# Gate matrix of a PEER layer: one of four weighted one-hot rows made on ScalarE instead of VectorE

## What is computed

```
expert_idx = take_along_axis(cand_idx, pos)      # i1 * 128 + i2, 8 x 16 = 128 pairs a token
gate = softmax(top_s)
u = w_down[expert_idx]
act = gelu(einsum("td,thkd->thk", x, u)) * gate
y = einsum("thk,thkd->td", act, w_up[expert_idx])
```

## Time and profile before

| what | value |
|---|---|
| median of 3 runs | 3774.1 us (3767.93 to 3777.16) |
| profiled execution | 3774.63 us, span 3772.9 us |
| mean granted clock of TensorE | 0.913 |
| gate matrix stage | first comparison at 1072.75 us, last Gelu ends at 1256.55 us |
| busy over the span | TensorE 3206.5 us, VectorE 2896.3 us, ScalarE 1722.9 us, GpSimd 938.3 us |

### The profile page before, as it was taken

How to read it: one execution, slowest core, us unless ns; L and a number is a source line. 1 busy time by engine, 2 the same in 40 slices (tenths; PEclk the granted TensorE clock), 3 DMA queues, 4 the chain that set the end, 5 groups by cost and what they waited for, 6 DMA issues and landing times. The chain is left out here.

```text
span 3772.9 us, 47355 instructions
## 1 busy us (share of the span) xinstructions
PE 3206.5 (85%) x16065; PEld 2717.1 (72%) x16065; DVE 2896.3 (77%) x3965; ACT 1722.9 (46%) x1905; POOL 938.3 (25%) x566
## 2 busy tenths in 40 slices
PE   4877559688888799999999756569999999999991
PEld 4877437588888788888888425457888887877881
DVE  5899673358979787787888233569999999998995
ACT  3222222323333333333333122168787888877782
POOL 4455100034521254444444000110101101111112
PEclk8888779899999899999999876589999999999996
DMA  3121002224344799898997201279999999998983
GB/s 104 45 67 34 1 10 102 95 95 145 132 163 179 287 354 345 328 333 338 347 343 272 93 9 51 82 278 351 358 357 361 348 355 363 356 366 349 357 341 127
DMA packets 198884, 851.15 MB, mean 226 GB/s; under 512 B 21232, under 2 KB 104960, under 8 KB 155584
## 3 DMA queue, kind: packets, MB, share of 16 engines
q1 hardware_dynamic: 170288, 698.66, 50.3%
q0 software_dynamic: 28496, 151.16, 9.9%
HBM read 808.20 MB, written 59.38 MB: 230 GB/s over the span
## 5 line engine op out<-in xcount | busy, mean ns | idle before, releaser
L2468 DVE TENSOR_TENSOR moe_w_lo<-all_raw,moe_w_hi 128x2048 fp32r<-128x2048 f32 x298 | 674.2, 2284 | 74.0 <-ACT moe_w_hi L2412 73.5
L2412 ACT ACTIVATE moe_w_hi<-all_raw 128x2048 fp32r<-128x2048 f32 x298 | 565.8, 1914 | 44.2 <-PE moe_GU L2383 29.7
L2383 PE MATMUL moe_GU<-moe_w_hi,moe_x_lo 128*128 128x512 f32 x1056 | 418.1, 396 | 0.0
L2381 PE MATMUL moe_GU<-moe_w_hi,moe_x_hi 128*128 128x512 f32 x1056 | 417.9, 396 | 0.0
L2382 PE MATMUL moe_GU<-moe_w_lo,moe_x_hi 128*128 128x512 f32 x1056 | 417.9, 396 | 0.0
L463 DVE SCALAR_TENSOR_TENSOR all_yT<-proj_gated,proj_taps,all_yT 128x512 f32<-128x512 f32 x240 | 266.4, 1110 | 8.5
L1100 POOL TENSOR_TENSOR score_wd_lo<-all_hT,score_wd_hi 128x1024 fp32r<-128x1024 f32 x52 | 139.5, 2709 | 528.5 <-ACT score_wd_hi L1147 528.5
L1618 DVE SCALAR_TENSOR_TENSOR experts_pair<-experts_pair,all_x_first 128x1024 f32<-128x1024 f32 x128 | 156.3, 1221 | 141.3 <-DMA experts_pair<-in_peer_pairs,experts_slot 141.3
L1467 POOL DMA_INDIRECT experts_pair<-in_peer_pairs,experts_slot x128 | 223.6, 1747 | 115.4 <-POOL experts_slot L1464 109.6
L1464 POOL COPY experts_slot<-all_pair_id 128x1 uint32 x128 | 153.3, 1197 | 331.5 <-DVE all_h L1630 300.4
L2382 PEld LDWEIGHTS moe_GU<-moe_w_lo,moe_x_hi 128*128 128x128 f32 x1056 | 198.8, 188 | 48.6
(11 more groups left out here) (442 smaller groups left out, 8382.7 us busy)
## 6 DMA issues: line engine op xcount, KB each, us to landing
all_raw<-in_w_moe SPq DMA_DIRECT2D x149, 2048.0 KB, 9.4
all_hT<-in_w_moe SPq DMA_DIRECT2D x49, 2048.0 KB, 9.3
all_wu<-in_peer_pairs SPq DMA_DIRECT2D x64, 1024.0 KB, 10.0
all_hT<-in_peer_wdT SPq DMA_DIRECT2D x76, 512.0 KB, 13.2
all_hT<-in_peer_wdT SPq DMA_DIRECT2D x13, 2048.0 KB, 7.9
peer_gates<-gates_out SPq DMA_DIRECT2D x6, 4096.0 KB, 11.3
experts_gt<-peer_gates SPq DMA_DIRECT2D x32, 768.0 KB, 10.2
all_hT<-in_w_in SPq DMA_DIRECT2D x40, 512.0 KB, 3.8
```

Of the source, the lines that this page charges most:

```text
L2381: pe.matmul(out, x_hi[:, kx, :], hi[:, k, :], start=False, stop=False)
L2383: mm = pe.matmul(out, x_lo[:, kx, :], hi[:, k, :], start=False, stop=(kx == KD - 1))
L2412: act.activation(w_hi[p % RING][:], piece_of(r, p), ACT.Copy).then_inc(w_high, 1)
L2468: dve.tensor_tensor(w_lo[p % RING][:], piece_of(r, p), w_hi[p % RING][:].bitcast(F32), ALU.subtract).then_inc(w_low, 1)
```

## The change

VectorE makes the weighted rows of tokens 0, 1 and 2 of a group only. That of token 3 comes from ScalarE in two operations: the distance |key 1 - count| (function Abs, scale -1, bias the key number, into a small ring `far` of two), and the tent relu(gate - gate * distance) (function Relu, scale the negated gate, bias the gate), which is the gate where the distance is 0, and 0 where it is 1 or more, as the gates are positive. VectorE negates all gates once at the start of the stage (`minus`, 128x384). ScalarE makes the distances of groups 0 to 4 and the tents of groups 0 to 3 before all else; then behind the copy of group n the distance of group n + 5 and the tent of group n + 4. TensorE waits for `tented` too. In the last batch ScalarE's loop is written out, so that it stops at the last group.

```diff
+        minus = s.sb("minus", [P, TD])
+        far = s.sb("far", [P, 2, NK])
...
             def _(dve):
                 shape = [P, U, NK]
+                dve.tensor_scalar(minus[:], c.idxT[:, 2, :], -1.0, None, ALU.mult).then_inc(negated, 1)
...
-                        for j in range(U):
+                        for j in range(U - 1):
                             mark = dve.tensor_scalar(hot[:, u, 0, j, :], c.count[:], c.idxT[:, 0, ds(at + j, 1)],
                                                      c.idxT[:, 2, ds(at + j, 1)], ALU.is_equal, ALU.mult)
...
                             pe.wait_ge(weighed, n + 1)
+                            pe.wait_ge(tented, n + 1)
                             pe.wait_ge(taken, n + 1)
...
+                def distance(n, u, first=False):
+                    if not first:
+                        act.wait_ge(tented, n - 1)
+                    act.activation(far[:, u % 2, :], c.count[:], ACT.Abs, scale=-1.0,
+                                   bias=c.idxT[:, 0, ds(n * U + (U - 1), 1)]).then_inc(spread, 1)
+
+                def tent(n, u):
+                    at = n * U + (U - 1)
+                    act.wait_ge(spread, n + 1)
+                    act.activation(hot[:, u % R, 0, U - 1, :], far[:, u % 2, :], ACT.Relu, scale=minus[:, ds(at, 1)],
+                                   bias=c.idxT[:, 2, ds(at, 1)]).then_inc(tented, 1)
+
+                def take(b, q, left=None):
                     for u in range(R):
-                        act.wait_ge(g_done, q * R + (R * per * b + u + R + 1))
+                        n = q * R + (R * per * b + u)
+                        act.wait_ge(g_done, n + (R + 1))
                         act.activation(out[:, b % 2, :, ds(q * (R * U) + u * U, U)],
                                        ps[:, u, :, :].rearrange("p t i -> p i t"), ACT.Copy).then_inc(taken, 1)
+                        if left is None or u + R + 1 < left:
+                            distance(n + (R + 1), u + 1)
+                        if left is None or u + R < left:
+                            tent(n + R, u)
...
                 act.sem_inc(gelued, 2)
+                act.wait_ge(negated, 1)
+                distance(0, 0, first=True)
+                for n in range(R):
+                    distance(n + 1, n + 1, first=(n == 0))
+                    tent(n, n)
...
-                    with act.Fori(1, per) as q:
-                        take(b, q)
+                    if b < BATCHES - 1:
+                        with act.Fori(1, per) as q:
+                            take(b, q)
+                    else:
+                        for q in range(1, per):
+                            take(b, q, R * (per - q))
```

More of the change, by code:

```diff
@@ L1257, in stage_gate_matrix @@
         ps = s.ps("ps", [P, R, U, NK])
-        (weighed, g_done, taken) = (s.sem(n) for n in ("weighed", "g_done", "taken"))
+        minus = s.sb("minus", [P, TD])
+        far = s.sb("far", [P, 2, NK])
+        (weighed, g_done, taken, negated, spread, tented) = (s.sem(n) for n in (
+            "weighed", "g_done", "taken", "negated", "spread", "tented"))
         saved = [s.sem(f"saved{b}") for b in range(2)]
@@ L1333, in split @@
                     act.activation(wd_hi[:, t % 2, :], wd[:, t % 2, :], ACT.Copy).then_inc(wd_h, 1)
-                def take(b, q):
+                def distance(n, u, first=False):
[9 more added lines that the diff above has]
+                def take(b, q, left=None):
                     for u in range(R):
-                        act.wait_ge(g_done, q * R + (R * per * b + u + R + 1))
+                        n = q * R + (R * per * b + u)
+                        act.wait_ge(g_done, n + (R + 1))
                         act.activation(out[:, b % 2, :, ds(q * (R * U) + u * U, U)],
                                        ps[:, u, :, :].rearrange("p t i -> p i t"), ACT.Copy).then_inc(taken, 1)
+                        if left is None or u + R + 1 < left:
+                            distance(n + (R + 1), u + 1)
+                        if left is None or u + R < left:
+                            tent(n + R, u)
                 act.sem_inc(taken, R)
                 act.sem_inc(gelued, 2)
+                act.wait_ge(negated, 1)
[3 more added lines that the diff above has]
+                    tent(n, n)
                 for b in range(BATCHES):
```

## The result

The changed kernel takes 3747.5 us (median of 6 runs, 3738.9 to 3754.5) against 3773.6 (6 runs, 3767.9 to 3777.2): ratio 0.9932, 95% interval 0.9917 to 0.9948, so 20 to 31 us less. The forecast was 3753 and -21, in a range from 3746 to 3764. Run again beside the kernel before it took 3750.7 (6 runs) against 3771.5 (17 runs), ratio 0.9949 (0.9934 to 0.9964); the two intervals meet at 0.993 to 0.995, 20 to 25 us.

The account below looks back on a forecast made before the run. VectorE was taken to bound the gate-matrix stage. Removed rows -24.7, negation +0.4, TensorE's lag +2.1 and slow clock +1.0 gave -21.2 us, from 3774.6 to 3753.4, said as 3753, range 3746 to 3764.

Parts of the forecast that it names:

- The bound: In the gate-matrix stage VectorE's 96 groups and 12 stalls set the pace, 30.17 us a batch before, 26.0 after.
- The removed rows: On VectorE, one of four weighted rows goes in each of 96 groups, at 0.257 us each: -24.7 us.
- ScalarE hidden: ScalarE's added distance and tent fit its idle time: 1.18 us a group, 21.6 a batch against VectorE's 26.0.
- The stalls: VectorE's 12 waits for GpSimd's low parts, 2.03 us each, stay; possible shrinking of 2 to 4 us kept for low end.
- The negation: VectorE negates the gates once, 128x384, before its first comparison: +0.4 us, all on the path.
- TensorE's lag at the end: After the last stall TensorE falls behind VectorE by 0.21 us a group over nine or ten groups: +2.1 us.
- The slow clock: After a stall's idleness TensorE may run at its 1.2 GHz level, 1.31 us more for one group: +1.0 us taken.
- rival 2: TensorE holds VectorE in the stage through two slow-clock spells a batch, some 8 us net lost: 3761 us, chance 0.12.
- 1 (ScalarE the mild bound): ScalarE paces the stage at 1.60 us a group, 28.7 a batch, saving 8.8 us: 3766 us, chance 0.10.
- 3 (a handoff at each operation): ScalarE pays a handoff at every operation, 1.86 us a group, +16 us: 3791 us, chance 0.05.
- 4 (table loads): Two table loads at each of ScalarE's 12 Gelus, 5.1 us a batch, leave no gain: 3774 us, chance 0.03.

Follow-up runs that it names:

- run 3: The changed kernel plus one more Abs of 128x128 a group on ScalarE, into a tile nobody reads: stage 161.36 us, 3750.2 us, ratio 0.9951.
- 3b: The changed kernel plus two more Abs of 128x128 a group on ScalarE, into a tile nobody reads: stage 184.37 us, 3772.2 us, one run.
- Run 2: The changed kernel with two of four weighted rows made by ScalarE instead of one: stage 193.59 us, 3785.6 us, ratio 1.0029.
- run 1: The changed kernel without ScalarE's distances and tents and without the negation, every fourth token's gates left out: stage 162.03 us, 3750.3 us, ratio 0.9938.
- Run 6: The kernel before, plus only the negation of the gates and ScalarE's wait for it: stage 184.16 us, 3768.6 us, one run.
- run 5: The changed kernel with each tent right behind its own group's distance on ScalarE: stage 161.67 us, 3749.4 us, ratio 0.9951.
- runs 7 and 8: Low parts made by VectorE instead of GpSimd: 7 on the changed kernel, 3741.9 us; 8 on the kernel before, 3758.7 us.

## Why the prediction was right

*The bound.* VectorE paces the stage, before and after: right, to 0.1 us a batch (26.06 for 26.0).

*The removed rows,* -24.7: the part from first comparison to last row shrank by 24.53. The price was the spacing of 0.257; the 336 ns that a record lasts would have made it 32 us.

*ScalarE hidden:* right in all of its parts. 1.16 us a group for 1.18, Abs 400 ns and Relu 489, a Gelu and a split held by the slack of four slots, and the end of the cover between run 3 (1.45 us, free) and 3b (1.74, not free). One small slip: by its own working the tent comes to 0.71 - 384 x 0.9 ns = 0.36 us and not 0.38. It measured 0.39. The Trainium skill's advice in "ScalarE: Activation LUTs", Rules for kernel authors, to keep relu and mul on VectorE holds for the price of the work (0.68 against 0.257 us) and fails for this kernel's time, since the dearer engine was idle. Run 2, where a second row of four moves and the time gets longer, is where it begins to hold.

*The stalls.* The prediction kept 2 to 4 us at the low end of its range for shorter stalls, should more of GpSimd's operation fall on a comparison. That reasoning fails. In the changed kernel GpSimd starts 0.04 us ahead of the row that it holds in one place and 0.48 in another, and in run 1 up to 0.68, and the stall is 2.04 to 2.09 us in all of these. What grows is GpSimd's own operation: 2.35, 2.79 and 3.01 us.

*The negation,* +0.4: 0.04 in truth. The step that failed is "all on the path": VectorE's first comparison had been held there by a signal, 0.36 us behind SP's load. Run 6 shows it by itself.

*TensorE's lag at the end,* +2.1: TensorE's last group starts 1.88 us behind VectorE's end, where 0.13 was (1253.97 in the timeline of before, against VectorE's end at 1253.84: a handoff), and the time from VectorE's end to the end of the stage grew from 2.71 to 4.33, by 1.62. The mechanism is as forecast. The size is not, as the last stall now falls on group 7 of the last batch: eight groups follow it, 8 x 0.21 = 1.7, where nine or ten were counted. Run 1, with ten groups behind its last stall, has 2.33.

*The slow clock,* +1.0: nothing. TensorE's granted clock was 0.50 from 1068 to 1072 and 0.60 in the next 2 us, and full from 1074 to the end in windows of 2 us; its idle time behind the first stall of a batch, 2.50 us in four of six batches before, is now between 1.47 and 1.75 us, as its lag covered part of the stall. What the prediction said against rival 2 is what happened. Why the clock stayed up isn't settled: in the kernel before it also fell behind an idle time of 1.82 us (the group before the slow one of the earlier trace rows), hardly longer than the 1.75 behind which it now stayed full, and the length of one idle time doesn't decide it: in run 3 the clock stayed full behind 1.97 us (to the group at 1134.10), in run 5 it fell to 0.50 (1138 to 1140) behind 1.95. No run here changes the idle time alone.

The terms as measured: -24.53 + 0.04 + 1.62 = -22.87, the stage's difference. The forecast -21.2 erred by 1.7 us: three terms were too high, by 1.0 (clock), 0.4 (negation) and 0.5 (lag), and the removed rows came 0.2 short. The time of the whole kernel fell by 26.1 us in the first measurement and by 20.8 in the second. How near either of them comes to -21.2 is partly luck, as a single profile of the same code scatters by several us outside the stage. The stage's 22.9 is what bears on the forecast.

*The rivals.* 1 (ScalarE the mild bound) didn't come; run 3 shows the room. 3 (a handoff at each operation) is refuted in its size: even in the order that provokes it (run 5), only the wait for the operation just ahead costs. It is 0.26 us, close to the handoff of 0.13 with the overlap of 0.10, but only once a group. 4 (table loads) has no row. By the Trainium skill, "ScalarE: Activation LUTs", Table sets, relu and abs are in every set; this trace agrees, with 96 of each between 12 Gelus and no load.

## What to carry to other kernels

If one engine is busy through a whole stage, read the price of its instruction from the distance of starts, and the room on the other engine per round of the loop. As long as the other engine's sum stays under the pacing engine's round, stalls included, even work that is nearly three times dearer there is free. Well beyond that point the round is the other engine's own sum (run 3b: 30.57 us a batch). Write down at which cost a group the cover ends: here 1.46 us, and the runs at 1.45 and 1.74 fell on either side. If the pacing engine stalls for another engine's work, try to give it that work: here a stall of 2.05 us went for an operation of some 1.2.

## What the runs showed of the hardware that was not expected

- While GpSimd subtracts 128x1024 fp32 elements, VectorE's 128x128 row that comes next stands until GpSimd is done. In the kernels before and after this costs 2.03 to 2.08 us, and 2.15 to 2.21 where the row had begun just ahead of GpSimd. A comparison that is under way goes through at its usual 0.68 us (before: comparison from 1084.57, GpSimd from 1084.90), and GpSimd's operation is the longer for it: 2.35 to 2.79 us in the two kernels, by how far it starts ahead of the row. It is not the kind of operation that protects the comparison. In run 2 two comparisons that started 0.35 and 0.55 us into GpSimd's operation were held like the rows, and lasted 2.56 and 2.38 us. The first of them:

```profile
1086.92 2.37 POOL L1298 TENSOR_TENSOR gates_wd_lo<-all_hT,gates_wd_hi 128x1024 fp32r<-128x1024 f32 x1 [5.76 <-ACT gates_wd_hi L1338]
...
1087.27 2.56 DVE L1285 TENSOR_TENSOR gates_hot<-all_count,all_idxT 128x512 f32<-128x512 f32 x1 [0.63 <-PE gates_ps L1312]
```

- The same subtraction lasts 1.22 us on VectorE, and makes the distance of two comparisons 1.13 to 1.24 us longer (runs 7 and 8).
- A wait on ScalarE for its own operation just ahead costs 0.26 us (run 5). For one further back it costs nothing: distance and tent are 0.29 us apart in the change, where the tent waits, as are two distances in run 3b that don't wait.
- With ScalarE saturated (runs 2 and 3b), the records of its operations get longer, from 0.60 us to some 0.8 for a copy and up to 1.12, but their spacing doesn't: copy to the next operation stays 0.48. The spacing is the price.
